# The third branch's attention weights transposed by VectorE's 32x32 blocks and a pass through DRAM, with their value products in the next group

## The reference

```python
def dilated_window_attention(q, k, v, dilation, half):   # 8 heads of 64
    s = jnp.einsum('bhrnqd,bhrnld->bhrnql', qb, kb) * (hd ** -0.5)
    s = jnp.where(valid, s, -1e30)
    lse = jax.nn.logsumexp(s, axis=-1)
    p = jnp.exp(s - lse[..., None])
    o = jnp.einsum('bhrnql,bhrnld->bhrnqd', p, vb)
    ...
for window, dil in ((128, 1), (512, 4), (2048, 16)):
    o_g, lse_g = dilated_window_attention(qc, kc, vc, dil, window // (2 * dil))
    ...
wts = jax.nn.softmax(jnp.stack(lses, axis=0), axis=0)
o_c = jnp.einsum('gbhs,gbhsd->bhsd', wts, jnp.stack(outs, axis=0))
y_c = o_c.reshape(B, S, BRANCH_W) * jax.nn.silu(c_g)
```

## Time and profile before

| | us |
|---|---|
| median of three runs | 1241.46 |
| the profiled execution, its own time | 1241.94 |
| its span in the trace | 1240.1 |
| TensorE busy | 1217.7 (98%) |
| GpSimd busy | 831.5 (67%) |
| VectorE busy | 690.3 (56%) |
| ScalarE busy | 439.9 (35%) |

### The profile page before, as it was taken

The page is one execution under the profiler, slowest core; times in us unless marked ns, Lnnn a source line. Parts: engine busy times, 40 slices in busy tenths (PEclk is TensorE's granted clock), DMA queues, the critical chain, the costliest instruction groups (busy, mean ns, idle before and its releaser), DMA issues.

```text
span 1240.1 us, 17610 instructions
## 1 busy us (share of the span) xinstructions
PE 1217.7 (98%) x5840; PEld 983.5 (79%) x5840; DVE 690.3 (56%) x1025; ACT 439.9 (35%) x791; POOL 831.5 (67%) x595
## 2 busy tenths in 40 slices
PE   7999999999999999999999999999999999999995
PEld 5887788778878887787888878887887788777884
DVE  6686227532753385677658741583247334648852
ACT  6325523542354145200253453145314532450012
POOL 5787377737762876677849753885388548857881
PEclk9999999999999999999999999999999999999998
DMA  6343233323332333374244332523252315336611
GB/s 240 103 115 117 94 101 106 111 94 102 109 104 93 119 95 121 127 267 153 90 154 145 86 107 75 170 82 105 72 152 88 117 51 152 102 103 232 206 68 68
DMA packets 51790, 148.61 MB, mean 120 GB/s; under 512 B 6560, under 2 KB 8096, under 8 KB 51360
## 3 DMA queue, kind: packets, MB, share of 16 engines
q1 hardware_dynamic: 28800, 103.04, 24.7%
q10 hardware_dynamic: 22944, 44.98, 11.9%
HBM read 114.45 MB, written 16.78 MB: 106 GB/s over the span
## 4 chain that ended last, share of the span: by engine, by line
PE 94%; DVE 3%; ACT 1%; issue 1%; DMA 1%; ACTq 0%; POOLq 0%; POOL 0%; DVEq 0%
PE proj L1075 54%; PE proj L1178 10%; PE turn L1313 4%; PE turn L1239 3%; PE score L1313 3%; PE score L1231 3%; PE score L1232 2%; PE mbank L1247 2%; PE obank L1247 2%; PE mbank L1313 2%; PE obank L1313 2%; PE proj L1093 1%; PE obank L1266 1%; PE mbank L1067 1%; DVE yl L1010 1%; PE turn L1170 1%
## 5 line engine op out<-in xcount | busy, mean ns | idle before, releaser
L418 POOL TENSOR_TENSOR wl<-raw_w,wh 128x512 fp32r<-128x512 f32 x352 | 503.5, 1452 | 31.7 <-POOL wh L409 31.7
L409 POOL TENSOR_SCALAR wh<-raw_w 128x1024 fp32r<-128x1024 f32 x176 | 215.9, 1227 | 290.4 <-issue 103.6
L1075 PE MATMUL proj<-hh,wh 128*128 128x512 f32 x1024 | 405.8, 396 | 0.5 <-DVE big L1037 0.5
L1075 PE MATMUL proj<-hh,wl 128*128 128x512 f32 x1024 | 400.5, 391 | 0.0
L1075 PE MATMUL proj<-hl,wh 128*128 128x512 f32 x1024 | 399.5, 390 | 0.0
L1075 PEld LDWEIGHTS proj<-hh,wh 128*128 128x128 f32 x1024 | 192.3, 188 | 42.5 <-issue 2.8
L1075 PEld LDWEIGHTS proj<-hh,wl 128*128 128x128 f32 x1024 | 192.2, 188 | 41.6
L1075 PEld LDWEIGHTS proj<-hl,wh 128*128 128x128 f32 x1024 | 192.5, 188 | 39.2
L528 ACT ACTIVATE six<-big 128x512 f32<-128x512 f32 x24 | 15.0, 626 | 202.9 <-DVE big L1037 202.9
L926 DVE CUSTOM_DVE_ANT_0 six<-score,lmask 128x512 f32<-128x512 f32 x64 | 43.2, 683 | 66.8 <-PE score L1232 66.8
L884 DVE TENSOR_TENSOR group<-big,group 128x512 f32<-128x512 f32 x24 | 37.5, 1615 | 73.2 <-ACT big L617 73.2
(11 more groups left out here) (199 smaller groups left out, 1880.9 us busy)
## 6 DMA issues: line engine op xcount, KB each, us to landing
raw_w<-weights SPq DMA_DIRECT2D x175, 512.0 KB, 3.3
gate_scratch<-gstage ACTq DMA_DIRECT2D x48, 256.0 KB, 2.1
six<-gate_scratch ACTq DMA_DIRECT2D x16, 768.0 KB, 5.3
big<-big ACTq DMA_DIRECT2D x64, 128.0 KB, 3.5
yh<-yh ACTq DMA_DIRECT2D x64, 128.0 KB, 2.4
big<-x_t SPq DMA_DIRECT2D x4, 512.0 KB, 6.4
big<-x_t SPq DMA_DIRECT2D x1, 2048.0 KB, 8.9
x_scratch<-big SPq DMA_DIRECT2D x1, 2048.0 KB, 7.3
```

Of the source, the lines that this page charges most:

```text
L409: pool.tensor_scalar(wh[:, slot, :, :], src, 1.0, 1.0, ALU.mult, ALU.mult).then_inc(pool_high.sem, 1)
L418: ins = pool.tensor_tensor(wl[:, slot, half, :], src[:, half, :], wh[:, slot, half, :].bitcast(F32), ALU.subtract)
L1075: last = pe.matmul(dst, a[:, slot, k, :], b[:, k, :], start=(k == 0 and a is wh and b is hh), stop=(k == KT - 1 and a is wl))
```

## The change

In branch C, PE no longer transposes and DVE no longer divides. ACT multiplies the exponentials by the reciprocal of their sum in place (`scale`), and DVE transposes the 32x32 blocks of the tile into `w` (`turn_32`), where two tiles of queries lie side by side. When both are there, SP writes `w` to a DRAM tensor in four transfers and reads it back in four, so that the blocks end up on the partitions of their keys (`send`): one such pass for each of four pairs m of tiles in a group. `w` holds one pair, so the transposes of the next pair wait until the transfers to DRAM of the last have landed (`sent`). C's tiles now come in the order of the heads (four tiles of head 0, then four of head 1).

C's value products (`third_values`) and DVE's last multiplication (`third_branch`) move into the next group: on PE between v1 and v2, on DVE ahead of the first use of the decays. For the last group of a layer they stand behind the loop. v0 and v1 are copied out later, since `v` is still in use, and v2 and v3 go to the score banks. On SP the first two passes stand ahead of the group's last weight load and the other two behind it, at the end of the group.

```diff
@@ SP @@
+            def send(G, m):
+                sp.wait_ge(*turned_32.at(G, 2 * m + 2))
+                for a in range(4):
+                    sp.dma_start(turned_d[m, :, :, a, :], w[32 * a:32 * a + 32, :, :].rearrange("i n s -> i (n s)").rearrange(
+                        "i (x j) -> i x j", j=64)).then_inc(sent.sem, 16)
+                if m == 0:
+                    sp.wait_ge(*c_parts.at(G, 1))
...
+                if m == 2:
+                    sp.wait_ge(*out_done.at(G, 3))
...
+                sp.wait_ge(*sent.at(G, 64 * (m + 1)))
+                for c in range(4):
+                    k, q = QB * (m // 2), 2 * P * (m % 2)
+                    sp.dma_start(big[32 * c:32 * c + 32, k:k + QB, q:q + 2 * P], turned_d[m, :, QB * c:QB * c + QB, :, :].rearrange(
+                        "i x a j -> i x (a j)")).then_inc(back.sem, 16)
...
                     for j in range(GU):
+                        if j == GU - 1:
+                            send(L * NG + i, 0)
+                            send(L * NG + i, 1)
                         sp.wait_ge(*split_done.at(L, i * GU + (last + 1)))
                         unit(L, i * GU + (4 + j), arrival(4 + j)[0])
+                    send(L * NG + i, 2)
+                    send(L * NG + i, 3)
@@ ACT @@
+                        if j >= 12:
+                            act.wait_ge(*turned_32.at(G, j - 11))
...
+                    def scale(n):
+                        act.wait_ge(*rs_ready.at(G, n + 1))
+                        act.activation(probs[:, n % 4, :], probs[:, n % 4, :], ACT.Copy, scale=rs[:, n + 8:n + 9]).then_inc(scaled.sem, 1)
...
-                    for u in range(4, 10):
-                        exp(u + 6)
-                        turned(u)
...
+                    for n in range(2 * QB):
+                        scale(n)
+                        if n < 6:
+                            exp(n + 10)
+                        if n == 1:
                             merge_gate(2)
...
+                        if n == 5:
                             merge_gate(3)
...
@@ DVE @@
+                    def inverse(n):
+                        dve.wait_ge(*exp_done.at(G, n + 9))
+                        dve.reciprocal(rs[:, n + 8:n + 9], sums[:, n + 8:n + 9]).then_inc(rs_ready.sem, 1)
...
+                    def turn_32(n):
+                        dve.wait_ge(*scaled.at(G, n + 1))
+                        if n < 2:
+                            dve.wait_ge(*turn_done.at(G, 4))
                         else:
+                            dve.wait_ge(*sent.at(G, 64 * (n // 2)))
+                        dve.transpose(by_quarter(w[:, :, :], n % 2), probs[:, n % 4, :].rearrange("p (k c j) -> p k c j", k=QB, c=4)).then_inc(turned_32.sem, 1)
...
+                    for n in range(2 * QB):
+                        inverse(n)
+                        if n:
+                            turn_32(n - 1)
+                        if n < 6:
+                            row_max(n + 10)
...
+                    turn_32(2 * QB - 1)
@@ PE @@
-                    for u in range(4, 10):
-                        if u % 2 == 0:
-                            scores(u // 2 + 3)
-                        fill(3 if u in (5, 7) else 4)
-                        turn_weights(u)
...
+                    scores(5)
                     fill(4)
+                    scores(6)
+                    fill(5)
+                    pe.wait_ge(*y_read.at(G, 2))
+                    mean_of(obank, 2)
+                    scores(7)
+                    fill(20)
...
+                        elif b == 2:
+                            third_values(i - 1)
...
+                def third_values(i):
+                    G = L * NG + i
+                    pe.wait_ge(*r_done.at(G, 1))
+                    pe.wait_ge(*back.at(G, 4 * 64))
...
```

More of the change, by code:

```diff
@@ L309, in build @@
         gloaded = [sig(f"gloaded{s}", 4 * 16) for s in range(2)]
+        sent = sig("sent", 4 * 64)
+        back = sig("back", 4 * 64)
         s_out = sig("s_out", 16)
@@ L574, in values_out @@
                         have(f"v{b}")
-                        free(act.activation(v[:, b, :], proj[b % 2][:, 0:3 * P], ACT.Copy, scale=rcol[:, b:b + 1] if first else 1.0))
+                        free(act.activation(v[:, b, :], (proj[b % 2] if first or b < 2 else score[b % 2])[:, 0:3 * P], ACT.Copy, scale=rcol[:, b:b + 1] if first else 1.0))
                     if first:
@@ new lines, in weights @@
+                        a, c = 2 * u, 2 * u + 1
+                        dve.wait_ge(*exp_done.at(G, c + 1))
+                        grp.did(dve.reciprocal(rs[:, a:a + 2], sums[:, a:a + 2]))
+                        grp.last()
+                        grp.did(dve.tensor_scalar(rs[:, c:c + 1], rs[:, c:c + 1], sc[:, 2:3], None, ALU.mult))
+                        grp.did(dve.tensor_scalar(w[:, u % 2, :], probs[:, a % 4, :], rs[:, a:a + 1], None, ALU.mult))
+                        grp.last()
+                        dve.scalar_tensor_tensor(w[:, u % 2, :], probs[:, c % 4, :], rs[:, c:c + 1], w[:, u % 2, :],
+                                                 ALU.mult, ALU.add).then_inc(w_ready.sem, 1)
@@ L1126, in _, with values @@
                 first_values()
+                def values(done, *products):
+                    for k in range(QB):
+                        for dst, cols, weights in products:
+                            last = pe.matmul(dst, v[:, k, cols], weights[:, k, :], start=(k == 0), stop=(k == QB - 1))
+                    last.then_inc(done.sem, 1)
+                def third_values(i):
+                    G = L * NG + i
+                    pe.wait_ge(*r_done.at(G, 1))
+                    pe.wait_ge(*back.at(G, 4 * 64))
+                    values(out_done, (mbank[0:HD, :], slice(2 * P, 2 * P + HD), wt1),
+                           (mbank[HD:P, :], slice(2 * P + HD, 3 * P), wt))
                 def group(i, first):
@@ L1240, in turn_weights @@
                         last.then_inc(turn_done.sem, 1)
-                    def values(ready, done, *products):
-                        pe.wait_ge(*wt_ready.at(G, ready))
-                        for k in range(QB):
-                            for dst, cols, weights in products:
-                                last = pe.matmul(dst, v[:, k, cols], weights[:, k, :], start=(k == 0), stop=(k == QB - 1))
-                        last.then_inc(done.sem, 1)
                     def mean_of(dst, n):
@@ L1297, in _ @@
                     group(i, False)
+                third_values(NG - 1)
                 with pe.Fori(0, 2) as half:
```

138 lines of the change are left out of this document (63 added, 75 removed).

## The result

The changed kernel takes 1336.61 us in the median of 4 runs (1335.14 to 1338.37); the kernel before, run with it on the same chip, takes 1241.61 (1240.56 to 1241.88). The ratio is 1.077 (95% interval 1.0757 to 1.0782): 95 us slower. The profiled execution took 1337.61 us, with a span of 1335.6.

The account below looks back on a forecast made before the run. TensorE was taken to bound the kernel, busy 1217.7 of 1240.1 us. 1241.9 + 139 (six groups of 16.4, two layer ends of 20.4) + 12 of clock = 1393, or 1392 as median; range of 8 in 10: 1305 to 1540.

Parts of the forecast that it names:

- the forecast's own range: Whole kernel: 1340 to 1455 us, from T of 6.2 to 8.7 and the ends of clock and transpose; chance 0.65.
- The rival with T = 5.4: Passes to DRAM: small pieces cost nothing, each pass as long as the exchange of halves; 1320 us, chance 0.15.
- T: Time from a DRAM pass's first issue to its landing: 7.5 us taken, 6.2 to 8.7; each us worth 32 in all.
- the signs that would show the sum wrong: At the passes to DRAM: the sum is wrong if `turn_scratch<-w` lands in under 4 or over 12 us.
- the clock's end: PE behind its wait at `gate()`: upper end of the lower clock's cost, 35 us in all where 12 was taken.
- the slow transpose: DVE's block transpose at 1.24 us instead of 0.7, making the sum some 30 us longer.
- C's values at a layer's end: `third_values` behind the loop: begins at 47.2 instead of 26.8, 20.4 us later, after a way back of 5.4.
- the slow rival: Passes to DRAM: small pieces cost up to the ceiling, T = 13 to 17, 1568 to 1696 us; chance 0.15.
- The landing to `gate()`: Group end: after the fourth landing SP issues the way back (2.7) and `up` (0.3), which lands 2.8 us later.
- The clock: PE's v1 behind the wait at `gate()` runs at a lower clock: 1.5 us per group, 12 in all.
- The order of PE's waits: In a group: 0.8 at third pair's scores, 5 at last scores, about 2 at m5, the rest of 20 at `gate()`.
- The turns: C's eight TensorE transposes per group go: 0.435 us each, 3.5 per group, 28 over eight groups.

Follow-up runs that it names:

- experiment 9: Changed kernel with second-layer gate stores cut to 8 rows of 128: 1327.2 us; the same edit with passes to DRAM as whole 4 KB rows: 1292.97 us.
- experiment 7: Changed kernel with passes to DRAM written as whole rows of 4 KB instead of 256 B pieces, so keys are read wrongly: 1302.17 us.
- Experiment 6: Changed kernel with 24 unread products on TensorE between v0 and gate(), in the groups of the loop: 1320.67 us.
- experiment 3: Changed kernel with the load of the next group's up issued ahead of the first pass instead of behind the fourth: 1288.09 us.
- experiment 2: Kernel before the change, with one of four TensorE transposes in each of C's eight turns of a group, three left out: 1219.76 us.
- experiment 1: Changed kernel without its passes through DRAM and the waits for them, so C's values read unturned keys: 1222.12 us.
- experiment 8: Changed kernel with the group's last weight load issued ahead of the first pass instead of ahead of the third: 1328.19 us.

## Why the prediction came out as it did

The sign, the cause and the order of the waits were right, and the time lies in the range of 8 in 10. But 1392 was 55 us too high, and 1337 lies just under the forecast's own range of 1340 to 1455. The rival with T = 5.4, at 1320, was nearer. Of the signs that would show the sum wrong, one came about: `turn_scratch<-w` lands 3.7 us after its issue, and under 4 was the mark. The upper end of the forecast's own range was also added up wrongly. T = 8.7 gives 1430 and the clock's end 23 more, 1453; the slow transpose, which the text counts in, would add its 30 and make 1483. Step by step, in the frame of one group (t = 0 at 379.3):

| step | predicted | measured |
|---|---|---|
| first pair in `w`, first pass issued | 5.4 | 5.4 |
| T, mean of four | 7.5 | 5.93 |
| between passes | 2.4, 2.4, 1.6 | 2.0, 2.5, 1.9 |
| fourth landing to `gate()` | 5.8 | 4.4 |
| `gate()` | 47.6 | 40.0 |
| C's values at a layer's end | 47.2 | 39.3 |
| clock, per group with a wait | 1.5 | 3.1 |
| block transpose | 0.7 | 0.695 |

- **The step that failed is the size of T**, 5.93 instead of 7.5 (5.92 over all 32 passes). It makes 4 x 1.57 = 6.3 of the 7.6 us by which `gate()` came earlier than forecast, in eight groups 50 us. Both halves of the term were too large. The base was taken from the exchange of halves, 5.4; alone the same bytes take 3.5 (experiment 9). And 38 ns for a piece came from the mean of a window with other packets in it. In the changed kernel the window of 2.5 us in the first pass has, in its rows of queues (packets, MB, share of 16 engines):

```profile
q1 hardware_dynamic: 1270, 0.31, 62.5%
```

  That is 0.625 x 16 x 2.5 us over 1270 packets, 19.7 ns each: the half that I had as lower end. 128 of them are 2.5 us on each engine, about the 2.6 that SP needs to issue the four transfers, so most of it can lie beside the issues, and experiments 7 and 9 show that the pieces cost 1.05 us where I had 2.1. What I had no term for, the gate stores and a weight load beside the passes, put 1.3 back: without that luck the forecast would have been further off. The slope was right: I had 32 us for each us of T, and experiment 7 took 34.4 us off with 1.02 less.
- **Pieces under 512 B** were the slow rival. The Trainium skill ("DMA: Bandwidth & Descriptors", Specifications) says they are written by read-modify-write. No doubling shows here: the passes took 4.8 us alone, and the 13.6 worked out from that rule is excluded. The trace of the changed kernel also has the time of each packet. In the median the 65,536 of 256 B took 18 ns, those of 516 B 28, of 1 KB 46, of 2 KB 84 and of 4 KB 159. A straight line through the last two gives 18 for 256 B, so the small pieces pay for a fixed part of some 9 ns each and for nothing that a piece of 516 B doesn't. (The packets of other sizes belong to other transfers, most of them loads.)
- **The landing to `gate()`** was 4.4 instead of 5.8: the way back is issued in 1.74 us, not 2.7, and `up` lands in 2.0, not 2.8. At the layer end the way back takes 4.1 (from its first issue at 547.49 to C's values at 551.60) instead of the 5.4 of the exchange.
- **The clock** cost twice my value, 3.1 in this group and 2.9 in the mean where PE waits 5 to 7.5 us: `gate()` itself, for which I had nothing, is 1.0 of it, v1 2.1. Experiment 6 shows 16 us for the loop. 2.0 more come at each layer end, in C's values.
- **The order of PE's waits**: 0.54 at the third pair's scores (predicted 0.8), 2.76 at the last scores (5), none at m5 (2), 6.1 at `gate()` (8 to 12). All are smaller with T. DVE's idle times ahead of its third, fifth and seventh block transpose were 4.8, 3.2 and 7.5, 5.1 in the mean of all 24, where I had some 7 for each. The wait at `gate()` is for `up` and not for `back`, as the working had it, and experiment 3 shows that `up`'s place alone carries 48.5 us.
- **The turns** were worth what I had: 28, and 28 to 29 by experiment 2.

The sum with the terms measured in this group: 5.2 + 3.6 + 3.1 = 11.9 per group, 71 for six (67 by the trace); 12.5 + 2.0 = 14.5 per layer end, 29 for two. Together 100, where 95 were measured. PE's share came out at 92% instead of 88: its idle time grew by 86 us and not by some 145.

What stays open: some 3 of the 9 us by which experiment 1 falls short of the turns' worth have no row. With short stores the fourth pass is still 0.3 to 0.4 longer than the second, for no reason that I can name. And what the full stores cost a pass of whole rows is uneven, 0.1 in the first and 1.5 in the fourth.

## What to carry to other kernels

A load that someone waits for must not stand in an issuing queue behind transfers that wait for others: one such load, 64.5 KB, was half of the loss, and moving it cost nothing. A serial chain of transfers is priced by its round trips, so ask first how many are in flight at once, and only then how large the pieces are: a second buffer alone gave 3 us here, whole rows 34, and the buffer, the order of the passes and the two loads moved ahead 94 together. And where the chain ends, look for work whose own inputs don't hang on what is waited for, or the wait only changes its name.

## What the runs showed of the hardware

- A block transpose of 128x512 f32 in 32x32 blocks with a strided output took 0.695 us on DVE (64 of them), as a plain operation with one tile in and one out. The Trainium skill ("VectorE: DVE Perf Modes", section on the three transpose paths) has 311 ns for 128x128 of 2-byte numbers; four times that, the 1.24 us of the estimate, did not show.
- Packets of 256 B from SBUF to DRAM took 18 ns each in the median of 65,536, and 19.7 by the busy share of a window. SP took 0.65 us to issue a transfer of 512 such pieces (2.60 for four, in a pass with no gate store beside it) and 0.43 for the same bytes as 32 rows (1.71 to 1.74 for four).
- Gate stores of 256 KB beside a pass of 512 KB made it 0.1 to 1.5 us longer in the mean of four groups, and the 512 KB weight load ahead of a pass 1.3 (experiment 8). With both, four issues took 4.0 us instead of 2.6.
- After a wait of 6 us PE ran the next 2 us at 0.50 of its clock and the 6.5 behind that at 0.65 in the mean. Filling that wait with products nobody reads gave back 2.7 us per group.
